# Weaving memory attention into the gate units that follow the memory's k and v, and reordering the first halves of block attention

## The reference, cut to what matters

```
q, kv, nsa_g, conv_in, q_mem, merge_g = split(h @ w_in)
o_nsa  = nsa_attention(q, compressed / selected / window k and v, gates)   # 16 heads of 64
o_conv = short_gated_conv(conv_in)
km, vm = split(rmsnorm(mem) @ w_mem_kv)           # 256 memory positions, 4 heads of 256
qm     = rmsnorm(q_mem);  km = rmsnorm(km)         # per head
pm     = softmax(qm @ km^T * 256 ** -0.5)
o_mem  = pm @ vm
g_nsa, g_conv, g_mem = split(sigmoid(merge_g))
x = x + (g_nsa * o_nsa + g_conv * o_conv + g_mem * o_mem) @ w_out
```

## Time and profile before

| | |
|---|---|
| median of 3 runs | 2965.48 us |
| the profiled execution's own time | 2964.67 us |
| its span | 2962.9 us |
| TensorE matmul busy | 2878.8 us (97%) |
| VectorE, ScalarE, GpSimd busy | 1302.3, 1141.5, 1113.9 us |
| mean granted TensorE clock | 0.989 of full |

### The profile page before, as it was taken

How to read it: one execution, slowest core, us unless ns; L and a number is a source line. 1 busy time by engine, 2 the same in 40 slices (tenths; PEclk the granted TensorE clock), 3 DMA queues, 4 the chain that set the end, 5 groups by cost and what they waited for, 6 DMA issues and landing times.

```text
span 2962.9 us, 33445 instructions
## 1 busy us (share of the span) xinstructions
PE 2878.8 (97%) x13394; PEld 2277.4 (77%) x13394; DVE 1302.3 (44%) x2055; ACT 1141.5 (39%) x1811; POOL 1113.9 (38%) x506
## 2 busy tenths in 40 slices
PE   8999989899999999999999999999999899999999
PEld 6888867766667757888887777888887577888887
DVE  4333244365656425433324345333337555533333
ACT  4322233355553533332224454323235465423323
POOL 3444433122224423444442223444444333444443
PEclk9999999799999999999999999999999999999999
DMA  4443232122212312232321112223322232232322
GB/s 146 151 143 122 90 109 86 50 75 75 75 63 100 107 50 81 98 96 96 110 90 64 58 50 71 94 99 102 108 90 86 93 114 101 93 100 97 117 89 82
DMA packets 83362, 275.51 MB, mean 93 GB/s; under 512 B 14183, under 2 KB 20583, under 8 KB 82568
## 3 DMA queue, kind: packets, MB, share of 16 engines
q1 hardware_dynamic: 73292, 257.10, 26.1%
q0 software_dynamic: 9440, 15.16, 1.5%
q10 hardware_dynamic: 476, 1.12, 0.1%
HBM read 271.13 MB, written 10.58 MB: 95 GB/s over the span
## 4 chain that ended last, share of the span: by engine, by line
PE 85%; DVE 10%; ACT 3%; issue 2%; DMA 1%; SPq 0%; POOL 0%; DVEq 0%; ACTq 0%
PE bank L446 21%; PE bank L448 21%; PE bank L447 21%; PE bank L599 3%; PE bank L603 3%; PE bank L601 3%; DVE prob L1758 2%; PE bank L809 1%; PE bank L626 1%; PE bank L665 1%; PE bank L750 1%; DVE tmp L1606 1%; PE bank L778 1%; PE bank L653 1%; PE bank L562 1%
## 5 line engine op out<-in xcount | busy, mean ns | idle before, releaser
L2163 POOL TENSOR_TENSOR w_lo<-raw,w_hi 128x1024 fp32r<-128x1024 f32 (+1 forms) x423 | 1076.4, 2546 | 1693.9 <-ACT w_hi L1101 1693.9
L1101 ACT ACTIVATE w_hi<-raw 128x1024 fp32r<-128x1024 f32 (+1 forms) x424 | 469.2, 1107 | 1298.3 <-PE bank L448 1199.6
L446 PE MATMUL bank<-a_hi,w_hi 128*128 128x512 f32 x1888 | 747.6, 396 | 21.0 <-DVE a_lo L1588 7.1
L448 PE MATMUL bank<-a_lo,w_hi 128*128 128x512 f32 x1888 | 737.8, 391 | 0.0
L447 PE MATMUL bank<-a_hi,w_lo 128*128 128x512 f32 x1888 | 737.6, 391 | 0.0
L446 PEld LDWEIGHTS bank<-a_hi,w_hi 128*128 128x128 f32 x1888 | 356.0, 189 | 108.7 <-issue 16.3
L447 PEld LDWEIGHTS bank<-a_hi,w_lo 128*128 128x128 f32 x1888 | 356.5, 189 | 77.4 <-issue 4.5
L448 PEld LDWEIGHTS bank<-a_lo,w_hi 128*128 128x128 f32 x1888 | 356.1, 189 | 74.5
L446 PE MATMUL bank<-h_hi,w_hi 128*128 128x512 f32 x704 | 273.9, 389 | 0.0
L447 PE MATMUL bank<-h_hi,w_lo 128*128 128x512 f32 x704 | 273.9, 389 | 0.0
L448 PE MATMUL bank<-h_lo,w_hi 128*128 128x512 f32 x704 | 273.9, 389 | 0.0
(11 more groups left out here) (307 smaller groups left out, 3496.2 us busy)
## 6 DMA issues: line engine op xcount, KB each, us to landing
raw<-in_w SPq DMA_DIRECT2D x360, 512.0 KB, 3.4
raw<-in_w SPq DMA_DIRECT2D x64, 704.0 KB, 4.0
bias_rows<-bias_table POOLq DMA_DIRECT2D x4, 2048.0 KB, 30.1
strip<-bias_rows SPq DMA_DIRECT2D x16, 448.0 KB, 4.2
cw<-in_cw POOLq DMA_DIRECT2D x4, 1024.0 KB, 5.6
terms<-forget_cumsum SPq DMA_DIRECT2D x8, 512.0 KB, 7.8
terms<-forget_cumsum SPq DMA_DIRECT2D x8, 384.0 KB, 6.7
x<-in_x_t SPq DMA_DIRECT2D x4, 512.0 KB, 7.5
```

The source lines that it names most:

```text
L446: mm(dst, high[:, w], hi[:, kbase + b], start=start and b == 0, stop=False)
L448: last = mm(dst, high[:, w], lo[:, kbase + b], start=False, stop=stop and b == nk - 1)
L1101: act(w_hi[v % 3][:, 0:nk * P], raw[v % 5][:, 0:nk * P], ACT.Copy).then_inc(sem("w_hi_ready"), 1)
L2163: eng.tensor_tensor(w_lo[v % 5][:, 0:nk * P], raw[v % 5][:, 0:nk * P], w_hi[v % 3][:, 0:nk * P].bitcast(F32), ALU.subtract).then_inc(sem(" ...
```

## The change

Two edits, in one kernel.

**Block attention's halves.** On ScalarE, both `exps` of a half now come before `cmp_exp` and `conv_gate`, and `ahead("conv", 0, 2h, 4)` stands behind `copies` instead of ahead of them, in both halves. On VectorE, in the first half, both `bias` come directly behind `cmp_bias`, and then `cmp_low` and `out(c - 1)`.

**Memory attention.** The 8 `gnsa` units move behind `memkv` in the stream of weights. `project("qmem")` directly follows `nsa`, its tiles go to a buffer `qm` of their own (the 8 tiles of `q_t` still hold block attention's output), and the second of its units waits until the last of these outputs is taken. `mem_attention` now has 8 steps, one for two heads and one query tile, woven into the 8 `gnsa` units: 4 matmuls of unit k, scores of step k (four matmuls of 256 columns), 10 matmuls, values of step k-1, the last 10, the transposes of step k. The values alternate between the two halves of the array's columns, with 128 columns each. The last values stand in the first `gmem` unit. ScalarE's step is two exponentials, the unit's `w_hi` copy, the sigmoid and the copy out of PSUM; VectorE's is minimum, the gate of unit k-1, division, and the output of step k-1. `om` and `phase_pad` are gone, `mprob` and `mprob_t` use old buffers.

```diff
 STREAM = [
-    ("qkv0", 20, K8), ("conv", 32, K8), ("gnsa", 8, K8), ("qmem", 8, K8), ("memkv", 16, K8),
+    ("qkv0", 20, K8), ("conv", 32, K8), ("qmem", 8, K8), ("memkv", 16, K8), ("gnsa", 8, K8),
     ("gmem", 8, K8), ("wo0", 8, K8),
@@ tensor, mem_attention
+                def scores(t):
+                    a, i = t // 4, t % 4
+                    if t:
+                        eng.wait_ge(sem("m_exped"), 2 * t)
+                    for p in range(2):
+                        for kc in range(2):
+                            ch = 4 * a + 2 * p + kc
+                            last = mm(bank[4][:, p * NMEM:(p + 1) * NMEM], qm[:, ch, i * P:(i + 1) * P], km[:, ch, :],
+                                      start=kc == 0, stop=kc == 1)
+                def turn(t):
+                    eng.wait_ge(sem("m_scaled"), 2 * t + 2)
+                    if t:
+                        eng.wait_ge(sem("m_copied"), t)
+                    for n in range(4):
+                        last = eng.transpose(bank[5][:, n * P:(n + 1) * P], mprob[t % 2][:, n * P:(n + 1) * P], ident)
+                def values(t):
+                    a = t // 4
+                    eng.wait_ge(sem("m_copied"), t + 1)
+                    if t:
+                        eng.wait_ge(sem("m_out_taken"), t)
+                    for r in range(4):
+                        for kt in range(2):
+                            for p in range(2):
+                                f = (2 * a + p) * 256 + r * HD
+                                last = mm(bank[6][64 * p:64 * p + 64, r * P:(r + 1) * P], vm[:, kt, f:f + HD],
+                                          mprob_t[t % 2][:, (2 * p + kt) * P:(2 * p + kt + 1) * P],
+                                          start=kt == 0, stop=kt == 1, skip_group_check=True)
+                eng.wait_ge(sem("tile_taken"), taken0["gnsa"])
                 eng.wait_ge(sem("vtok_done"), v0["sb_qkv"])
+                for k in range(NCH):
+                    gate = gate_unit(k)
+                    advance(gate, 4)
+                    scores(k)
+                    advance(gate, 10)
+                    if k:
+                        values(k - 1)
+                    advance(gate)
+                    turn(k)
+                u = U0["gmem"]
+                for k in range(NCH):
...
+                    if k == 0:
+                        advance(gate, 12)
+                        values(NCH - 1)
+                    advance(gate)
-            tiles_by_four("gnsa", a_hi, a_lo, "tile_taken", taken0["gnsa"])
-            project("qmem", a_hi, a_lo, midway=lambda: mean("mem", NMEM, 7))
+            project("qmem", a_hi, a_lo, midway=lambda: mean("mem", NMEM, 7),
+                    begun=lambda: eng.wait_ge(sem("n_out_taken"), NCH))
@@ scalar, nsa
                         exps(h, 0)
+                        exps(h, 1)
                         if br == 0:
                             cmp_exp(c)
-                        exps(h, 1)
-                        ahead("conv", 0, 2 * h, 4)
-                        if br == 0:
                             conv_gate(c)
                         copies(h)
+                        ahead("conv", 0, 2 * h, 4)
                         ahead("conv", 0, 2 * h + 1, 4)
@@ scalar, mem_attention
+                for t in range(NCH):
                     eng.wait_ge(sem("m_min"), t + 1)
                     if t >= 2:
                         eng.wait_ge(sem("m_turned"), t - 1)
+                    for p in range(2):
+                        at = slice(p * NMEM, (p + 1) * NMEM)
+                        act(mprob[t % 2][:, at], bank[4][:, at], ACT.Exp, scale=-1.0, bias=stat[:, 2 * t + p:2 * t + p + 1],
+                            accum_out=stat[:, 16 + 2 * t + p:17 + 2 * t + p]).then_inc(sem("m_exped"), 1)
+                    ahead("gnsa", 0, t, 4)
+                    eng.wait_ge(sem("unit_done"), u + t + 1)
...
+                    act(act_t[t % 2][:, :], bank[t % 2][:, :], ACT.Sigmoid).then_inc(sem("sigmoid_done"), 1)
                     eng.wait_ge(sem("m_turned"), t + 1)
...
+                    act(mprob_t[t % 2][:, :], bank[5][:, :], ACT.Copy).then_inc(sem("m_copied"), 1)
@@ vector, nsa
                     cmp_bias(c)
+                    bias(2 * c, 0)
+                    bias(2 * c, 1)
+                    cmp_low(c)
                     if c:
                         out(c - 1)
-                    bias(2 * c, 0)
-                    cmp_low(c)
-                    bias(2 * c, 1)
                     scale(2 * c, 0)
@@ vector, mem_attention
+                for t in range(NCH):
+                    low(t)
+                    if t:
+                        gated(t - 1)
+                    high(t)
+                    if t:
+                        out(t - 1)
+                gated(NCH - 1)
+                out(NCH - 1)
@@ gpsimd
-            rests(U0["conv"] + 3, U0["gnsa"] + 3)
+            rests(U0["conv"] + 3, U0["qmem"] + 3)
             eng.wait_ge(sem("conv_done"), NCH)
             eng.wait_ge(sem("n_out_taken"), NCH)
             eng.dma_start(memx[:, :, :], mem_t).then_inc(sem("mem_in"), 16)
```

More of the change, by code:

```diff
@@ L724, in mem_attention @@
[L724 to L748, removed]
-                    for kt in range(2):
-                        last = mm(bank[r][64 * par:64 * par + 64, :], vm[:, kt, mh * 256 + r * HD:mh * 256 + (r + 1) * HD],
-                                  mprob_t[:, kt, :], start=kt == 0, stop=kt == 1, skip_group_check=True)
-                last.then_inc(sem("m_valued"), 1)
+                u, g = U0["gnsa"], gates0["gnsa"]
@@ L1855, in high @@
                 def high(t):
-                    wait("m_exped", t + 1)
-                    own(eng.reciprocal(stat[:, 16 + t:17 + t], stat[:, 16 + t:17 + t]))
-                    eng.tensor_scalar(mprob[t % 2][:, :], mprob[t % 2][:, :], stat[:, 16 + t:17 + t], None, ALU.mult)\
-                        .then_inc(sem("m_scaled"), 1)
-                def out(a):
-                    wait("m_valued", 2 * a + 2)
-                    for r in range(4):
-                        eng.tensor_copy(om[:, 4 * a + r, :], bank[r][:, :]).then_inc(sem("m_out_taken"), 1)
@@ L1865, in mem_attention @@
-                low(0)
-                low(1)
-                for t in range(4 * MH):
-                    high(t)
-                    if t + 2 < 4 * MH:
-                        low(t + 2)
-                    if t == 9:
-                        out(0)
-                out(1)
-            def gnsa():
-                tk = taken0["gnsa"]
-                def body(i):
-                    for k in range(4):
-                        wait("sigmoid_done", gates0["gnsa"] + 4 * i + k + 1)
-                        own(eng.tensor_tensor(act_t[k % 2][:, :], col(q_t, 4 * i + k), act_t[k % 2][:, :], ALU.mult))
-                        eng.tensor_tensor(col(mixed, 4 * i + k), col(mixed, 4 * i + k), act_t[k % 2][:, :], ALU.add)\
-                            .then_inc(sem("tile_taken"), 1)
+                    wait("m_exped", 2 * t + 2)
@@ new lines, in high, with out @@
+                    own(eng.reciprocal(stat[:, 16 + 2 * t:18 + 2 * t], stat[:, 16 + 2 * t:18 + 2 * t]))
+                    for p in range(2):
+                        v = mprob[t % 2][:, p * NMEM:(p + 1) * NMEM]
+                        eng.tensor_scalar(v, v, stat[:, 16 + 2 * t + p:17 + 2 * t + p], None, ALU.mult)\
+                            .then_inc(sem("m_scaled"), 1)
+                def out(t):
+                    a, i = t // 4, t % 4
+                    wait("m_valued", t + 1)
+                    eng.tensor_copy(qm[:, 4 * a:4 * a + 4, i * P:(i + 1) * P],
+                                    bank[6][:, :].rearrange("p (r n) -> p r n", n=P)).then_inc(sem("m_out_taken"), 1)
@@ L2129, in _ @@
             nsa()
-            gnsa()
             wait("mem_in", 16)
```

89 lines of the change are left out of this document (41 added, 48 removed).

## The result

The changed kernel takes 2925.76 us (2924.95 to 2926.91, 4 runs) against 2965.30 us in the same job (2963.71 to 2966.88, 4 runs): ratio 0.9867, 95% interval 0.9855 to 0.9879. The forecast was 2925.9. The span fell from 2962.9 to 2923.1 us.

What follows compares the result with a forecast made beforehand. TensorE, busy 97% of the span, was taken as the bound. From the profiled 2964.67 us, -19.4 (block attention) and -20.2 (memory attention with clock) give 2925.1; the runs' median stood 0.8 higher, so 2925.9, range 2918 to 2943.

Steps and rivals of the forecast that it cites:

- Part A: Block attention: moving the `w_hi` copy behind `copies` starts GpSimd's subtraction after VectorE's divisions; -19.4 us, 2.42 a head pair.
- The three late places: Block attention's transposes: start 1.46 us late in the window half; second tens 0.54 (window) and 0.42 (selected) late.
- The first rival: Block attention: the transposes' wait moves instead of going, time 2945.3 us, or 2933.6 if partly; chance 0.11.
- The selected half: Block attention: reordered exponentials and bias additions bring no gain and no loss, with about 1 us to spare.
- Part B: Memory attention woven into gate units: 37.7 us against 56.16, -18.5; with the clock's -1.7, -20.2 us.
- the flat 0.10 for each change: Woven step: every inserted piece pays two changes of kind at 0.10 us each; 48 changes, 4.8 us.
- The pairing: Woven values: alternating column halves makes two matmuls cost one; 1.96 us a step with changes, upper bound 3.70.
- The third rival: Woven values: pairs don't overlap when 16 stand in a row; 1.74 us more a step, +13.9, 2939.8; chance 0.05.
- The second rival: Woven step: GpSimd's subtraction stops division and gate multiply, chain 1.5 us late a step, +12, 2937.9; chance 0.07.
- The clock: `gmem`: a 3.4 us stretch at half clock goes, since woven TensorE does not idle before it; -1.7 us.
- The fourth rival: Woven stretch: TensorE's granted clock falls to the lower level and stays; +79.7 us, 3005.6; chance 0.03.
- The rule on mode changes: Woven step: by the skill only values pay, 16 changes, 1.6 us, a sum 3.2 lower; the forecast rejected this.

Runs made afterwards that it cites:

- a_only: Kernel before with only block attention's new ScalarE and VectorE order, memory attention as before: 2942.58 us, ratio 0.9932.
- move_only: Kernel before with only the `w_hi` copy (`ahead`) moved behind `copies` in both halves, VectorE's order as before: 2945.21 us, ratio 0.9941.
- order_only: Kernel before with block attention's other reorderings (`cmp_exp`, `cmp_low`, `out`), the `w_hi` copy left where it was: 2967.38 us, ratio 1.0011.
- unpaired: Changed kernel with the woven values no longer alternating between column halves, one head's four matmuls standing together: 2934.05 us, ratio 0.9894 to the kernel before.
- paired: Kernel before with memory attention's values made for two heads at once, alternating column halves, nothing woven: 2951.92 us, ratio 0.9958.
- after_again: Changed kernel repeated without any edit, as base for kernels beside it: 2926.03 us, ratio 0.9870 to the kernel before.
- b_only: Changed kernel with block attention's old ScalarE and VectorE order put back, memory attention woven: 2944.95 us, ratio 0.9940 to the kernel before.
- behind_turn: Changed kernel with scores of step k+1 directly behind the transposes of step k, at the gate units' border: 2924.46 us, ratio 0.9866 to the kernel before.

## Why the prediction was right, point by point

The total was off by 0.1 us, closer than its terms, whose errors partly cancelled.

- **Part A, -19.4 forecast.** By stage -20.2, by `a_only` 20.2. The working had 2.42 us a pair; the trace has 42.00 less 39.48, 2.52. The 0.10 is the change that the working put ahead of the transposes (0.33) and that isn't there: they follow the unit after 0.23. The three late places are gone as named, and the margin of 0.1 us for the second division held: the divisions end at 718.64 (717.37 plus 1.27), and the second ten are due at 717.68 plus 1.05, 718.73. The first rival (the wait moves) falls. The release order rests on one moved copy, as `move_only` shows.
- **The selected half, "no gain and no loss".** Right for the change as a whole, but for a reason that the working didn't have. The new order by itself delays the second ten by 0.52 us a pair (`order_only`), since all four divisions then come behind the stall. The move takes the stall away, and with it the cost. The step that I took as neutral is neutral only with the other one.
- **Part B, what comes: 4.52 us a step forecast, 10.0 from unit to unit.** The trace has 9.78, so 4.3. Add to each piece what the matmul behind it takes over its usual 0.23. Scores are then 1.54 plus 0.19 (1003.99 to 1004.41), 1.73 against 1.94 forecast. Transposes are 0.35 plus 0.09, 0.44 against 0.62. Values are 1.90 plus 0.11, and 0.09 more at the step into them (1006.24 to 1006.56), 2.10 against 1.96. The steps into scores and transposes are 0.22 and 0.24, as within a unit. So the term that was wrong is the flat 0.10 for each change. Scores and transposes cost what the working had for them without a change (1.74 and 0.42), and only the values pay, 0.34 a step where the working had 0.20. Eight steps are 1.5 us shorter than forecast.
- **The pairing, 1.96 instead of 3.70.** Right in kind, and both ways round: `unpaired` loses it and `paired` wins it alone. The third rival falls. The estimate from the Trainium skill's 81 ns a matmul ("TensorE: Matmul & The Clock Gate", "Back-to-back issue gap"), 2.6 us for a step's values, was too high: 32 records take 1.90.
- **The waits.** The first gate unit stood 1.96 us behind the last two matmuls on `sqtmp`, where the scores had stood 0.95 behind them: 1.0 more, as forecast. The last values waited 0.42, forecast 0.5. `qmem`'s start cost 0. The division of a woven step ends at 1007.99, due 1010.87 for the next transposes: slack 2.9, forecast 2.7. ScalarE, then VectorE, in that step:

```profile
1004.83 1.28 ACT L1315 ACT_TABLE_LOAD   x1
1006.12 0.48 ACT L1315 ACTIVATE sqsum<-bank,stat 128x256 f32<-128x256 f32 x1
```

```profile
1007.38 0.61 DVE L1876 TENSOR_SCALAR sqsum<-sqsum,stat 128x256 f32<-128x256 f32 x2
```

The chain is the one that was forecast: the table load follows the copy, the exponentials follow the load, and the division takes 0.61 us for both heads. GpSimd's subtraction runs from 1002.49 to 1004.86 and is over before it, as the forecast had it. The second rival falls.
- **The clock, -1.7.** The two low stretches of the earlier trace rows are gone from memory attention and `gmem`, but one of the same length stands behind `wo0`'s wait: +1.6 us there. It isn't the chance of one execution: the repetition's trace (`after_again`) has it behind the same wait, from 1125.6 on, and so has `b_only`. But idle time ahead of it is not enough to explain it: `behind_turn` and `unpaired` have the same gap there and go on at full clock (below, two stretches of `behind_turn`, busy times and clock as in the earlier trace rows; 15 matmuls in 3.4 us, where the changed kernel had 9). What decides it stays open. The old memory attention varies as well: two such stretches from `memkv` to `wo0` in the traces of the kernel before and of `move_only`, one in `a_only` and `order_only`. So the term of 1.7 was the place of one such stretch in one kernel's trace, and I should have put it in the spread. Against it stand the steps, 1.5 us shorter than forecast, and part A's 0.8, so the sum came out. That it came out to 0.1 us is luck.

```profile
1119.60:1122.87 3.27, 1.36 (x6) 0.49 (x4) 2.48 (x4) 0.63 (x1) 0.00 (x0) 1.00 0.00 0
1122.87:1126.27 3.40, 3.40 (x15) 2.84 (x16) 1.87 (x4) 2.10 (x3) 1.21 (x1) 1.00 0.37 114
```

- **The fourth rival** (a low clock in the woven stretch) falls: granted 1.00 over 79.74 us.
- **The rule on mode changes.** The Trainium skill's "TensorEngine Tiling (Array Packing)", "Key Properties", says that a change of the tiling mode drains TensorE; by the prediction's reading only the values would pay. The prediction said that the trace does not agree. That reading failed: it took a late matmul behind a piece for a charge, where it is time of the piece itself. The traces agree with the rule as to who pays (scores 1.73 and transposes 0.44 a step, 1.74 and 0.42 without a change; values 0.34 on top), and `behind_turn`, which by the rule saves nothing, saves 0.02 us a step at most. With the working's 0.10 for each of the two changes at the values a step would be 9.57, with the measured 0.34 for both 9.71; the trace has 9.78. What the 0.34 consists of stays open.

## What to carry to other kernels

Ask of every small VectorE instruction on a chain what GpSimd does beside it: here one ScalarE copy decided when GpSimd started, and moving that copy behind five others was worth 17.5 us by the ratio in 8 pairs (20.4 by the stage in the traces, 333.34 to 312.90). Where two matmuls write different column halves of the array, issue them alternately; as an edit of one loop that was worth 14.0 us in the trace (12.5 by the ratio), two thirds of the 21.6 that the rebuilt stage brought. Before you charge a change of kind, add up the piece and the matmul behind it: the late start there can be the piece's own time. And measure each half of a reordering alone: one that looks neutral can be harmful, and covered by its neighbour.

## What the runs showed that was not expected

- A VectorE product of 128x4 elements took 2.27 us beside GpSimd's subtraction, 0.17 without it. GpSimd's instruction took 2.38, so what is lost follows its length and not that of the one it catches. The Trainium skill's "SBUF — State Buffer", section "Who interferes with whom", says that the two engines share a pair of ports under an exclusive lock; this case's trace agrees.
- Two float32 matmuls on different column halves overlap wholly at 512 columns: 32 records in 7.01 us, where 16 of one half take 7.01 too. With 128 columns in a woven step 32 records take 1.90 us alternating and 3.25 not. The Trainium skill's "TensorEngine Tiling (Array Packing)", section "Key Properties", says that tiles can load and multiply in parallel; the traces agree where the instructions alternate between the tiles or stand at the border of two groups.
- Merging two inserted groups into one saved next to nothing (9.76 to 9.78 us a step against 9.78).
- A stretch of 3.4 us at half clock stands behind an idle gap in both traces of one kernel and is absent behind the same gap in another (`wo0` in the changed kernel and in `behind_turn`). Differences of 1.6 us between traces can be just that.
